# Issuing the fourth expert's gate-up load ahead of two state stores on the SyncE queue

## The reference, cut to what matters

```python
for l in range(DEPTH):                      # DEPTH = 2
    yp, bp, sp = mixer_block(yp, zero_buf, 0, zero_state, pos_p, *mix_w)
    ys, bs, ss = mixer_block(ys, cache_pool[l], n_prev_s, state_ret[l], pos_s, *mix_w)
    yp = hier_moe(yp, *moe_w)
    ys = hier_moe(ys, *moe_w)
...
for e in range(N_EXPERTS):                  # N_EXPERTS = 16, 1024 -> 256 -> 1024
    act = jax.nn.silu(hf @ w_gate[e]) * (hf @ w_up[e])
    y = y + (act * gates[:, e:e + 1]) @ w_down[e]
```

## Time and profile before

| | |
|---|---|
| median of 3 runs | 810.37 us (810.21 to 812.56) |
| the profiled execution | 810.1 us |
| its span in the profile | 808.3 us |
| PE / DVE / ACT / POOL busy | 98% / 74% / 59% / 41% of the span |
| granted TensorE clock, mean | 0.996 |
| first expert stage in the span | about 232 to 376 us |
| second expert stage | about 628 to 772 us |

### The profile page before, as it was taken

The page is one execution under the profiler, slowest core; times in us unless marked ns, Lnnn a source line. Parts: engine busy times, 40 slices in busy tenths (PEclk is TensorE's granted clock), DMA queues, the critical chain, the costliest instruction groups (busy, mean ns, idle before and its releaser), DMA issues.

```text
span 808.3 us, 11933 instructions
## 1 busy us (share of the span) xinstructions
PE 792.4 (98%) x4092; PEld 628.5 (78%) x4092; DVE 601.0 (74%) x951; ACT 478.4 (59%) x816; POOL 331.7 (41%) x225
## 2 busy tenths in 40 slices
PE   9999999999999999999999999999999999999995
PEld 6887788878757888888588787888776678888861
DVE  5445655575789999999754456646658899999986
ACT  5633333612578888887663432444335798888874
POOL 0015996310042355664100199925012234656530
PEclk9999999999999999999999999999999999999998
DMA  8832223224959999998753322222379699999967
GB/s 295 288 117 66 78 66 118 105 79 150 409 187 386 375 362 377 398 370 296 273 187 104 86 73 71 66 80 91 99 296 346 240 416 347 387 377 396 342 226 287
DMA packets 57295, 188.17 MB, mean 233 GB/s; under 512 B 10862, under 2 KB 11886, under 8 KB 49036
## 3 DMA queue, kind: packets, MB, share of 16 engines
q1 hardware_dynamic: 44476, 156.56, 53.7%
q0 software_dynamic: 10368, 23.09, 7.7%
q10 hardware_dynamic: 2400, 7.87, 2.6%
HBM read 172.99 MB, written 29.39 MB: 250 GB/s over the span
## 4 chain that ended last, share of the span: by engine, by line
PE 55%; DVE 29%; issue 8%; DMA 6%; ACT 2%; DVEq 0%; SPq 0%; POOL 0%; ACTq 0%; POOLq 0%
PE ps L499 13%; PE ps L503 10%; PE ps L502 10%; DVE gul L2198 9%; DVE dnl L2203 7%; DVE hgTl L2214 4%; PE ps L501 3%; DMA back<-y_d 2%; PE ps L1483 2%; PE ps L1485 2%; PE ps L1484 2%; DVE y L2223 2%; DMA y_d<-y,rowidx 2%; PE ps L1462 2%; DVE act L2235 1%
## 5 line engine op out<-in xcount | busy, mean ns | idle before, releaser
L911 POOL DMA_INDIRECT y_d<-y,rowidx x32 | 118.2, 3695 | 121.6 <-DVE y L2223 114.5
L499 PE MATMUL ps<-wh,hT 128*128 128x512 f32 x408 | 163.5, 401 | 0.2
L2198 DVE TENSOR_TENSOR gul<-wgu,eh 128x1024 fp32r<-128x1024 f32 x128 | 150.7, 1222 | 0.1
L2189 DVE SCALAR_TENSOR_TENSOR wl<-raw,gcol,wh 128x512 fp32r<-128x512 f32 x80 | 78.5, 983 | 75.8 <-ACT wh L1133 75.7
L1164 ACT ACTIVATE eh<-wgu 128x1024 fp32r<-128x1024 f32 x128 | 128.5, 1057 | 4.0 <-PE ps L1485 3.9
L503 PE MATMUL ps<-wh,lT 128*128 128x512 f32 x313 | 122.4, 391 | 0.0
L502 PE MATMUL ps<-wl,hT 128*128 128x512 f32 x313 | 121.9, 390 | 0.0
L1483 PE MATMUL ps<-eh,hgTh 128*128 128x512 f32 x240 | 96.6, 402 | 0.4 <-issue 0.4
L1485 PE MATMUL ps<-eh,hgTl 128*128 128x512 f32 x240 | 93.8, 391 | 0.0
L1484 PE MATMUL ps<-gul,hgTh 128*128 128x512 f32 x240 | 93.5, 389 | 0.0
L1133 ACT ACTIVATE wh<-raw,gcol 128x512 fp32r<-128x512 f32 x80 | 57.3, 719 | 60.3 <-PE ps L501 56.2
(11 more groups left out here) (277 smaller groups left out, 1612.6 us busy)
## 6 DMA issues: line engine op xcount, KB each, us to landing
wgu<-in_gate_up SPq DMA_DIRECT2D x64, 1024.0 KB, 12.3
wdn<-in_w_down SPq DMA_DIRECT2D x64, 512.0 KB, 14.3
raw<-in_w_in SPq DMA_DIRECT2D x79, 256.0 KB, 2.7
raw<-in_w_out SPq DMA_DIRECT2D x32, 256.0 KB, 3.0
back<-y_d SPq DMA_DIRECT2D x16, 512.0 KB, 6.1
s<-in_state_ret POOLq DMA_DIRECT2D x8, 512.0 KB, 4.1
xn_d<-xf ACTq DMA_DIRECT2D x8, 512.0 KB, 7.6
x_in<-in_x_cols SPq DMA_DIRECT2D x8, 288.0 KB, 4.9
```

The source lines that it names most:

```text
L499: pe.matmul(out, both, w_h, start=first, stop=False)
L911: pool.indirect_dma_start(out=y_d, out_offset=bass.IndirectOffsetOnAxis(ap=rowidx[:, 1, e:e + 1], axis=0), in_=y[s][:, :], in_offset=None, ...
L2189: ve.scalar_tensor_tensor(out=wl[S % SPL][:, :], in0=raw[S % RAW][:, :], scalar=gcol[:, 0, L, s % KC:s % KC + 1], in1=wh[S % SPL][:, :].bi ...
L2198: ve.tensor_tensor(gu_pair(gul, gul3, e, s, p), gu_pair(wgu, wgu3, e, s, p), gu_split(e, p)[:, :].bitcast(F32), ALU.subtract).then_inc(glo, 1)
```

## The change: what it does

In each layer SP issues the two gate-up transfers of the fourth expert as soon as the first gather has landed, ahead of the two late stores. Before, they were issued behind the landing of these stores and of the other two gathers. A wait for the fourth late matmul step (`skv_mm`) is added ahead of them, since the buffer overlays what these steps read. The down transfers stay where they were, behind the stores' landing.

```diff
                 sp.wait_ge(xn_st, 16 * NT * (L + 1))
                 sp.wait_ge(lg_mm, 3 * (L + 1))
                 sp.wait_ge(gat[0], 16 * used(L, 0, 0))
+                sp.wait_ge(skv_mm, 6 * L + 4)
+                load_gu(L, AHEAD, 0)
                 for j in (1, 0):
                     sp.wait_ge(s_late, 4 * L + (4, 3)[j])
                     sp.dma_start(o["new_ret_sample"][L, LATE + j], s_out[j][:, :, :]).then_inc(late_st, 16)
                 for s in range(3):
                     sp.wait_ge(gat[s], 16 * used(L, s, 0))
                 sp.wait_ge(late_st, 64 * (L + 1))
-                load_gu(L, AHEAD, 0)
                 load_dn(L, AHEAD, 0)
 
                 load_gu(L, 6, 0, after=0)
```

## The result

The changed kernel is slower: median 819.24 us (814.57 to 822.99, six runs) against 810.36 us (809.73 to 812.83, six runs), a ratio of 1.0102 with a 95% interval of 1.007 to 1.0133. The prediction was 810.3 us, no change. The runs also spread more than before, 8.4 us instead of 3.1. The profiled execution, 814.57 us with a span of 812.8, is the fastest of the six, so the trace shows the loss at its mildest.

The account below looks back on a forecast made before the run. DVE, full in both layers' expert loops, was taken as pacemaker, with PE full in the stretch ahead. All terms were 0 in both layers, against 810.1 us profiled and a median of 810.37: forecast 810.3 us, range 808.9 to 812.3.

Parts of the forecast that it names:

- the stores have landed at about 247.2 (246 to 249): Late stores behind the gate-up loads on SP's queue: 3.7 MB through by 246.0, plus 1.2 us; down transfers issued then.
- my start of 236.45: SP's forecast issue of the first layer's gate-up transfers, 6.0 us earlier than 242.46 before.
- The rate: DMA traffic from 237.1 on: 3.7 MB of loads, stores and gathers at 416 GB/s, taking 8.9 us, to 246.0.
- The tail: 1.2 us between the bytes being through (241.2) and SP going on (242.46) before the change, added to the stores' landing.
- The added wait: SP's wait for `skv_mm`, ahead of the gate-up loads: met by 235.95, before SP's 236.45, so cost 0.
- the cover: Expert 5's second half lands at 276.9, ACT reads it at 277.6: 0.7 us, plus ACT's 1.2 us idle each round.
- tied to finished matmuls, not to this place: SP's loads at the last scatter (6.00 us) and read back (5.47 us), said of whether these could shorten.
- my own price: Each us that the stores land after 250.2 costs 1 us per layer in the expert loop.
- my second rival: Late down transfers starve the expert loop: slower, 251.4 gives +2.4 us, 252 gives 813.9 us; chance 4%.
- X: Time of the stores' landing, until which SP stands still: stream behind above 248.3, ACT's slack used up at 250.2.
- The gather rival: Loads hold the second gather's signal, PE waits 0.4 to 1.4 us per layer: 811 to 813 us; 5% for passing 0.3%.
- The faster rival: Earlier load shortens DVE's idle ahead of its loop, 0.97 us per layer, 808.4 us if all vanished; over 0.3%: chance 4%.

Follow-up runs that it names:

- The doses: Kernel before, nothing moved, SP held by a PE event ahead of the fourth expert's down load, three lengths: 811.94, 817.89 and 821.36 us.
- the late dose: Kernel before, SP held ahead of the fourth expert's down load until expert 0's first down matmuls are done (out at 251.78): 821.36 us, ratio 1.014.
- The spread slots: Token slots dealt out over all 128 partitions: kernel before 809.11 us, the change 809.20, stores first 808.53, longest hold ahead of the down load 809.45.
- the middle hold: Kernel before, SP held ahead of the fourth expert's down load until expert 1's gate-up matmuls are done (out at 249.74): 817.89 us, ratio 1.0077.

## Why the prediction was wrong

**The step that failed** is "the stores have landed at about 247.2 (246 to 249)". They held SP until 250.36 in the first layer; in the second the 15.9 us from issue to issue would be 252.3 from my start of 236.45. Two terms were mis-sized. The rate: I took 416 GB/s; from 238 to 245 us of the changed kernel the queues moved (MB, share of 16 engines)

```profile
DMA packets 314, 2.13 MB, mean 304 GB/s; under 512 B 43, under 2 KB 43, under 8 KB 65
...
q1 hardware_dynamic: 266, 2.04, 89.8%
```

304 GB/s with the engines 90% busy. The sign of it stood in my own row: 1.65 MB in the 5.2 us from 243 to 248.2 at a share of 88%. At 304 GB/s the 3.7 MB take 12.2 us, to 249.3, and with the tail of 1.2 the sum gives 250.5: in the first layer the rate alone accounts for the miss. The tail: I took 1.2 us. From 248 to 249 in the first layer q1 and q0 ran at 22.0% and 27.1% of 16 engines, and from 648 to 649 in the second at

```profile
q1 hardware_dynamic: 12, 0.04, 9.1%
```

with the second store out for 14.2 us. And the frame, bytes ahead over a mean rate, does not carry over: with half the load bytes ahead the landing stayed where it was. The landing went with the last engine to finish, not with the mean.

The added wait, which I put at 0, was 1.1 us in the profiled execution, and the issue came 0.8 us late. That was the half clock of this execution; in the two kernels with the stores on ScalarE's queue and with the gathers held, which have the same wait, SP's issue came at 236.41 and 236.50, as I had forecast, with no such wait. This term stands.

**The second failed step** is the cover, and it weighs more. I found the tightest one, 0.7 us at expert 5's second half, plus ACT's 1.2 us, and took it that a lag passed there was over; of the loads at the read back I wrote that they are "tied to finished matmuls, not to this place". With the landings as they came, 250.36 and 252.3, my own price gives 0.2 + 2.1 = 2.3 us, 812.6. Measured are 819.24. The doses show what was missing: in a loop with the DMA engines 97% busy a lag can stay in the backlog to the layer's end and make the read back late too (9.01 us for 5.47 in the late dose). The spread slots take the price of the change and of the late hold away, so where the gathered rows lie decides how long the lag lasts. That the engines which serve those rows have no slack is the likely reason, but it is inferred.

**What held.** The mechanism that won was my second rival, given 4%. Its threshold, X = 250.2 for the first cost, was too late: 247.0 costs nothing, 249.7 costs 0.8%. Its slope, 1 us per layer for each us beyond, was about right: from 249.74 to 251.78 the median rises by 3.5 us, 1.7 per layer or 0.85 for each us. But at 249.74, where I had 0, the loss is already 6.6 us. The likelihood rested on X alone, to which I gave 4 us of margin; my own 247.2 lay at most 2.5 us ahead of a loss. The gather rival did not occur: PE does not wait for the second or third gather in any stage of the changed kernel, and the loss goes when the wait is moved, with the traffic as it was. The faster rival did not occur either.

**Left open:** which DMA engine is the last, and why it lags (it does with and without gathers, and with spread slots); why a fresh stream of loads runs at some 200 to 300 GB/s at first; and whether the spread slots work through the load of single engines. The profile gives the engines only together. The Trainium skill (DMA: Bandwidth & Descriptors, Latency and other measured facts) notes that engines 7 and 15 are usually slower than the rest; the one or two engines seen last here could fit, but no run here shows which they are. Why single executions of the changed kernel range over 8 us is not shown either. Landings that vary (13.1 and 15.9 us from issue to issue in one execution) are not needed for it: the middle hold, which ends with a PE event, ranges over 11.7 us.

## What to carry to other kernels

A wait on a DMA queue's issuer costs what stands behind it. Before a transfer is put ahead of one whose landing is awaited there, move the wait behind the loads that don't need it, or keep the awaited transfer first: either made this change free. Take a landing time from rows with the same traffic beside it on the DMA engines, not from bytes over a rate that was read elsewhere. If the engines are nearly full in the loop behind (97% here), count a lag once in the loop and once more where the layer's results are read back. And look where sparse gathers put their rows: here that alone decided whether a hold of 8 us cost 10 us or nothing, though the mean share of the engines in the loop (97% from 248 to 368 us with packed and with spread slots) gave no sign of it.

## What was not expected of the hardware

- Dealing 72 of 128 gathered rows over all partitions halved the landing time of unrelated weight loads late in the first layer's loop, from 14.9 to 7.4 us, with the same loads to move, and the kernel gained 0.3%.
- Two 512 KB stores issued behind 2 MB of loads, behind 1 MB, or on another queue beside them were all awaited until 250.0 to 250.4; issued just ahead of the same 2 MB, until 243.6.
- The last microsecond of such a landing ran at 6% to 9% of 16 engines, the worth of one engine or little more.
